# TensorE's convolution taps of a two-block model: fp32 products with one diagonal, or three fp32r products with rounded and remainder diagonals

## The chip, the cores and the metric

One core of one Trainium2 chip runs the whole program as one launch. The metric is the device time of the execution in microseconds, as the median of several runs of the kernel on one chip; less is better. Beside the runs there is one profiled execution, whose trace gives each instruction's start, length and engine.

## The reference, cut to what matters

The model has 1024 tokens of width 1024 and consists of three mixers with norms around them. The second, odd_mixer, is the one that the change touches:

```python
proj = h @ w_in                                   # 1024 -> 3 * 1024
a, b, gate = split(proj)
glu = a * sigmoid(b)
conv = depthwise_conv(glu, dw_w)                  # causal, 31 taps for each of 1024 channels
cf = conv + dw_b
cn = layer_norm(cf) * ln_g + ln_b
y = (silu(cn) * silu(gate)) @ w_out
x = x + rms_norm(y) * post_norm
```

Before it stands a mixer of windowed attention and pooling, after it a block with a third projection (to 3080 columns, with meta tokens in front), attention over all tokens, an output projection and a feed-forward part of 4096. All is computed in float32.

## The kernel before, in words

Activations lie with channels on the 128 partitions and tokens along the free axis, as 8 groups of 128 channels (KD = 8). From the first output projection up to the third input projection the tokens are worked in two halves of 512 (h = 0 and 1), so that one half's projection runs beside the other half's norms. The order of all work is written out by hand, engine by engine; engines wait for each other by semaphores, and each engine takes its own instructions in order.

**Projections.** An fp32 product is made of three fp32r ones: weights and activations are split into a rounded part (WH, XHM) and a remainder (WL, XLM), and `three` (L808) multiplies rounded by rounded, rounded by remainder and remainder by rounded. A job of one half is 8 channel groups by three matmuls of 128x512, 24 in all (half_job). Jobs of the third projection, first half, are "front jobs" (front_job): each covers the 16 meta tokens and 512 others as two pieces of 264 columns, 48 matmuls, in a ring bank and in one of banks 6 and 4. A PSUM ring of four banks holds the results of the jobs. A job p waits for `w_ready` to reach p + 1.

**Weights.** They pass through three slots in the order WORDER. SP loads the raw weights of job p; GpSimd issues a DMA of the rounded ones (`high`, L687) when job p - 3 has run, and computes the remainder (`low`, L694) of job p - 1. GpSimd's loop over p is: high(p), low(p - 1), additions due at p (`add_tap`, L749), diagonals due at p.

**The convolution** is shared by three engines. VectorE makes six of the eight groups by multiply-and-add, a tap at a time (`conv`, L2106 to L2110). Group 5 is made of products by ScalarE (`tap_products`, L1533) that GpSimd adds (L749). Group 4 is TensorE's: a tap is a matmul of the glu's columns, shifted by j, with a diagonal of 128x128 that holds the tap of each channel (`run_taps`, L1062), summed in bank 6. GpSimd makes a diagonal of the identity and a column of TAPW (`diagonals`, L738), in batches of 6, 5, 5, 5, 5, 5; a batch waits until the batch two before it has run, and lies in the first half's part of YG. ScalarE takes bank 6 with its bias (`group_out`, L1593).

**Where the taps stand.** First half: the batches run after jobs 8, 10, 12 and 14 of the second projection's first half (P_IN1A + i) and after jobs 0 and 2 of its second half (P_IN1B + i). Second half: all six batches run one after another between the gate jobs (P_GATEB + k) and the front jobs (P_IN2A + c). TensorE then makes five front jobs, the sum over channels for the mean (`mean1`, L1044, bank 5), three more front jobs, and the second output projection's second half.

**What stands around it.** On ScalarE: `sigmoid_b` takes the b part of a glu (L1540), half_hi rounds an activation (L1411), silu_gate takes a gate job (L1600), gate_b is a gate and then the products of group 5 that are due, front_copy takes an even front job as two copies of 264 columns (L1674, L1675). On VectorE: glu (L2094) multiplies in the a part, add_output (L2065, L2067) adds a normed output, scaled_lo (L2082, L1884) makes the third projection's inputs after the norm's broadcast (`half_wide`, L917, in the gates' job 5), front_product (L2239) takes an odd front job, mids (L2121) subtracts the mean. VectorE's order at the place is: scaled_lo for the first half, taps 12 to 30 of group 3, all of group 6, front_product(0), taps 0 to 13 of group 7, front_product(1), the rest of group 7, mids. Front job 2 waits for front_copy(0), front job 3 for front_product(0), which frees its second bank.

## Time and profile before

| what | value |
|---|---|
| median of 3 runs | 2202.93 us (2198.22 to 2207.03) |
| the profiled execution | 2204.82 us, span 2203.0 us |
| TensorE busy | 2128.3 us, 97% of the span |
| VectorE busy | 1116.0 us, 51% |
| ScalarE busy | 506.0 us, 23% |
| GpSimd busy | 760.3 us, 35% |
| mean granted TensorE clock | 0.982 |

The span runs from the first to the last instruction, and the execution's own time lies 1.8 us above it. Lines such as L808 are lines of the kernel before. "Busy" leaves out register, branch, semaphore and DMA-issuing instructions; matmuls overlap in the pipeline, so a row's mean length of one matmul is longer than its pace. In rows of a timeline the columns are start and length in us, engine, line, operation, output and inputs, count, and in brackets the engine's idle time before it and what ended it.

### The profile page before, as it was taken

What the parts mean: (1) busy time and instruction counts of PE and PEld (TensorE: products, weight loads), DVE (VectorE), ACT (ScalarE), POOL (GpSimd) and SP (SyncE); (2) the same over time, 40 slices, a digit from 0 to 9 for tenths busy, and PEclk for the clock granted to TensorE, in tenths of its full rate; (3) what the DMA queues carried; (4) which work ended last, traced back from release to release, by engine and by line L of the source; (5) the groups of instructions that cost most, each with busy time, mean ns of one, the idle gap of its engine ahead of it and who ended that gap; (6) DMA issues with size and microseconds to landing.
All of it is one profiled execution on the core that took longest, in us unless ns stands there. A gap on an engine that the chain in (4) does not pass through costs nothing.

```text
span 2203.0 us, 24066 instructions
## 1 busy us (share of the span) xinstructions
PE 2128.3 (97%) x9720; PEld 1675.2 (76%) x9720; DVE 1116.0 (51%) x1463; ACT 506.0 (23%) x832; POOL 760.3 (35%) x606
## 2 busy tenths in 40 slices
PE   7999999999999998989998999999999999999997
PEld 6887877777777767778886556777888888888886
DVE  6137563779999888151563676352322323313223
ACT  3002553421224413220111554111110100101102
POOL 3221015567767853434243000222222222222220
PEclk9999999999999998999999999999999999999999
DMA  4432017444544523447225442222222222222222
GB/s 178 138 116 72 25 60 246 172 153 143 176 160 154 171 96 115 157 151 246 77 79 142 90 92 78 101 96 77 96 96 96 96 96 96 96 96 96 96 96 105
DMA packets 71086, 259.85 MB, mean 118 GB/s; under 512 B 8961, under 2 KB 9217, under 8 KB 70209
## 3 DMA queue, kind: packets, MB, share of 16 engines
q1 hardware_dynamic: 40064, 148.69, 21.6%
q0 software_dynamic: 29808, 108.54, 13.7%
q8 instruction: 77, 1.26, 0.2%
q10 hardware_dynamic: 1104, 1.10, 0.2%
q14 instruction: 33, 0.26, 0.0%
HBM read 230.80 MB, written 12.65 MB: 111 GB/s over the span
## 4 chain that ended last, share of the span: by engine, by line
PE 59%; issue 28%; POOL 8%; DVE 4%; ACT 1%; DMA 1%; POOLq 0%; DVEq 0%; ACTq 0%
PE PS L808 55%; POOL WL L694 6%; DVE PS L2108 3%; PE PS L1062 2%; POOL WH L687 1%; DMA WH<-weights 1%; DVE OT L2511 0%; PE PS L917 0%; PE PS L1271 0%; PE PS L909 0%; ACT SQH L1533 0%; ACT PS L1618 0%; PE PS L1160 0%; DVE PS L2141 0%; ACT VX L1723 0%
## 5 line engine op out<-in xcount | busy, mean ns | idle before, releaser
L808 PE MATMUL PS<-XHM,WH 128*128 128x512 f32 (+1 forms) x1976 | 690.2, 391 | 24.9 <-DVE XLM L1884 12.3
L808 PE MATMUL PS<-XLM,WH 128*128 128x512 f32 (+1 forms) x1976 | 674.0, 382 | 0.0
L808 PE MATMUL PS<-XHM,WL 128*128 128x512 f32 (+1 forms) x1976 | 670.6, 381 | 0.0
L687 POOL DMA_DIRECT2D WH<-weights x207 | 119.2, 576 | 1323.7 <-PE PS L808 1305.5
L694 POOL TENSOR_TENSOR WL<-WRAW,WH 128x1024 fp32r<-128x1024 f32 x207 | 502.0, 2425 | 28.7 <-DMA WH<-weights 24.3
L808 PEld LDWEIGHTS PS<-XHM,WH 128*128 128x128 f32 x1976 | 368.5, 190 | 117.7 <-issue 22.9
L808 PEld LDWEIGHTS PS<-XLM,WH 128*128 128x128 f32 x1976 | 376.1, 190 | 79.8 <-issue 3.1
L808 PEld LDWEIGHTS PS<-XHM,WL 128*128 128x128 f32 x1976 | 375.5, 190 | 75.2
L2108 DVE SCALAR_TENSOR_TENSOR PS<-G,TAPW,PS 128x512 f32<-128x512 f32 x348 | 262.7, 755 | 11.7
L2489 DVE TENSOR_TENSOR X<-X,PS 128x1024 f32<-128x1024 f32 x64 | 78.2, 1222 | 243.5 <-PE PS L808 243.5
L2479 DVE SCALAR_TENSOR_TENSOR TM<-PS,RBM 128x1024 f32<-128x1024 f32 x32 | 39.1, 1225 | 246.4 <-PE PS L808 246.4
L1846 ACT ACTIVATE TM<-TM 128x1024 f32<-128x1024 f32 x32 | 33.9, 1061 | 550.3 <-DVE TM L2479 550.3
L808 PE MATMUL PS<-AL,WH 128*128 128x512 f32 x512 | 159.6, 393 | 0.0
L808 PE MATMUL PS<-AH,WH 128*128 128x512 f32 x512 | 158.8, 391 | 0.0
L808 PE MATMUL PS<-AH,WL 128*128 128x512 f32 x512 | 158.2, 390 | 0.0
L808 PEld LDWEIGHTS PS<-AH,WL 128*128 128x128 f32 x512 | 96.1, 188 | 22.0
L808 PEld LDWEIGHTS PS<-AL,WH 128*128 128x128 f32 x512 | 96.2, 188 | 20.9
L808 PEld LDWEIGHTS PS<-AH,WH 128*128 128x128 f32 x512 | 96.2, 188 | 20.3
L1229 PE MATMUL PS<-PT,VX 128*128 128x512 f32 (+4 forms) x224 | 86.0, 486 | 5.1 <-ACT PT L1773 5.1
L2472 DVE TENSOR_TENSOR AL<-TM,AH 128x1024 fp32r<-128x1024 f32 x32 | 84.3, 2655 | 1.1 <-ACT AH L1848 1.1
L749 POOL TENSOR_TENSOR RBM<-RBM,SQH 128x512 f32<-128x512 f32 x58 | 74.9, 1291 | 23.0 <-ACT SQH L1533 21.7
L1893 DVE TENSOR_TENSOR PS<-PS,SQH 128x512 f32<-128x512 f32 x60 | 41.6, 695 | 65.3 <-ACT SQH L1420 64.4
(253 smaller groups left out, 2084.8 us busy)
## 6 DMA issues: line engine op xcount, KB each, us to landing
WRAW<-weights SPq DMA_DIRECT2D x207, 512.0 KB, 3.5
WH<-weights POOLq DMA_DIRECT2D x207, 512.0 KB, 4.5
XTOK<-x SPq DMA_DIRECT2D x8, 512.0 KB, 7.6
x_kept<-X SPq DMA_DIRECT2D x4, 1024.0 KB, 7.6
X<-x_kept SPq DMA_DIRECT2D x8, 512.0 KB, 5.1
x_kept<-X SPq DMA_DIRECT2D x8, 512.0 KB, 8.6
X<-x_kept SPq DMA_DIRECT2D x2, 2048.0 KB, 9.6
out<-OT SPq DMA_DIRECT2D x8, 512.0 KB, 2.6
```

What stands on the lines that cost most here:

```text
L687: g.dma_start(WH[:, u, :], weights[WORDER[p]]).then_inc(w_hi[u], 16)
L694: g.tensor_tensor(WL[:, u, :], WRAW[:, u, :], WH[:, u, :].bitcast(F32), ALU.subtract)\
L749: g.tensor_tensor(dst, SSUMH[1], SQH[:, 1, i % 2, :], ALU.add).then_inc(tap_added, 1)
L808: m = nc.tensor.matmul(dst[:, a:b], w, v[:, a:b], start=first and n == 0, stop=last and n == 2)
L1062: m = nc.tensor.matmul(bank(6), diagonal(b, i - TAP_BATCH[part]), G1[:, c, h * HALF + j:(h + 1) * HALF + j], start=i == 0, stop=i == TAPS - 1,
L1229: m = nc.tensor.matmul(o[:, q0 - half * HALF:q0 - half * HALF + w], VX[0:keys, j, c, HD * e:HD * e + P], PT2[n % 3][0:keys, a:a + w], star ...
L1846: nc.scalar.activation(TM[:, j % 2, :], TM[:, j % 2, :], ACT.Square).then_inc(a_sq, 1)
L1893: v.tensor_tensor(so_far if k < KD - 1 else SSUMH[h], so_far, SQH[:, h, k % 2, :], ALU.add).then_inc(h_added[h], 1)
L2108: then(v.scalar_tensor_tensor(out=acc, in0=src, scalar=tap, in1=acc, op0=ALU.mult, op1=ALU.add))
L2472: v.tensor_tensor(AL[:, g % 2, j, :], TM[:, j % 2, :], AH[:, g % 2, j, :].bitcast(F32), ALU.subtract).then_inc(a_split, 1)
L2479: v.scalar_tensor_tensor(out=TM[:, j % 2, :], in0=slot(use + j), scalar=0.0, in1=RB[:], op0=ALU.max, op1=ALU.mult).then_inc(evacuated, 1)
L2489: v.tensor_tensor(X[:, e, :], X[:, e, :], slot(use + e), ALU.add).then_inc(evacuated, 1)
```

## The change

The tap as a float is split like the weights and activations of the projections. TAP2 holds, for the 31 taps of group 4, the rounded value and the remainder side by side (in the space of SMALL). ScalarE rounds the glu's columns into a strip (`tap_highs`): 542 columns as two strips of 286 (EDGE), and GpSimd subtracts the remainders (`tap_lows`). They lie in groups 4 to 7 of the first half's part of YG; the diagonals in groups 0 to 3. A tap is three fp32r matmuls: rounded diagonal by rounded strip, rounded by remainder, remainder by rounded; each reads its 512 columns as two pieces of 256, one in each strip. The product of the two remainders is left out.

A batch now has 4 taps (the last 3), so there are 8 in a half. GpSimd makes the four diagonals of two taps (two rounded, two remainders) in one two-input product of 128x512 with repeated elements, 16 instructions a half. tap_highs(0) stands on ScalarE behind the rounding of the second half's activations for the second projection, tap_lows(0) on GpSimd at P_IN1A + 8 behind low; the batches of the first half run on TensorE after jobs 10, 12, 14 and then 0, 2, 4, 6, 8. For the second half tap_highs(1) stands behind gate_b(4), tap_lows(1) at P_GATEB + 5, and the eight batches run in pairs behind front jobs 0 to 3, summed in bank 5. The waits for the inputs and for the first half's group stand before the front jobs; the wait for the second half's group stands before the mean. group_out(0) moves behind the fifth sigmoid of the second half, group_out(1) before the third front_copy.

The diff, with unchanged lines left out:

```diff
--- before.py
+++ after.py
@@ -68,7 +68,8 @@
...
 GLU_ORDER = (4, 5, 0, 1, 2, 3, 6, 7)
-TAP_BATCH = (0, 6, 11, 16, 21, 26, TAPS)
+TAP_BATCH = (*range(0, TAPS, 4), TAPS)
+NBATCH = len(TAP_BATCH) - 1
...
@@ -220,7 +221,9 @@
...
         RR = fixed("RR", [8, P])
+        o_small = top[0]
         SMALL = fixed("SMALL", [P, 96])
+        TAP2 = at("TAP2", [P, TAPS, 2], o_small, F32R)
         area = top[0]
...
@@ -241,6 +244,9 @@
...
         YG = at("YG", [P, KD, S], area + 33728)
+        YGR = at("YGR", [P, KD, S], area + 33728, F32R)
+        DIAG = at("DIAG", [P, KD, S // P, P], area + 33728, F32R)
+        EDGE = HALF // 2 + TAPS - 1
         SQH = at("SQH", [P, 2, 2, HALF], area + 66496)
...
@@ -368,6 +374,8 @@
...
         tap_added = sem("tap_added")
+        tap_hi = sem("tap_hi")
+        tap_lo = sem("tap_lo")
         diag_ready = sem("diag_ready")
...
@@ -500,9 +508,12 @@
...
-        def diagonal(b, n):
-            n += 6 * (b % 2)
-            return YG[:, n // 4, (n % 4) * P:(n % 4 + 1) * P]
+        def diagonal(b, n, e):
+
+            return DIAG[:, 2 * (b % 2) + n // 2, 2 * (n % 2) + e, :]
+
+        def tap_part(e, side):
+            return YGR[:, 4 + 2 * e + side, 0:EDGE]
...
@@ -723,20 +734,33 @@
...
+            def tap_lows(n):
+
+                c, h = TAP_GROUPS[n]
+                if n == 0:
+                    pool.wait_ge(tap_hi, 1)
+                    g.tensor_tensor(TAP2[:, :, 1], TAPW[:, c, :], TAP2[:, :, 0].bitcast(F32), ALU.subtract)\
+                        .then_inc(tap_lo, 1)
+                    pool.wait_ge(tap_lo, 1)
+                for side in range(2):
+                    first = h * HALF + side * HALF // 2
+                    pool.wait_ge(tap_hi, 2 + 2 * n + side)
+                    g.tensor_tensor(tap_part(1, side), G1[:, c, first:first + EDGE], tap_part(0, side).bitcast(F32),
+                                    ALU.subtract).then_inc(tap_lo, 1)
+
             def diagonals(b):
...
-                if b == 0:
-                    pool.wait_ge(taps_in, 16)
-                    pool.wait_ge(h_new[0], KD)
-                if b == 6:
-                    pool.wait_ge(h_new[0], 2 * KD)
+                n, part = divmod(b, NBATCH)
+                h = TAP_GROUPS[n][1]
                 if b >= 2:
                     pool.wait_ge(taps_run, b - 1)
-                (c, h), part = TAP_GROUPS[b // 6], b % 6
-                for i in range(TAP_BATCH[part], TAP_BATCH[part + 1]):
-                    j = taps_of(h)[i]
-                    g.tensor_scalar(diagonal(b, i - TAP_BATCH[part]), IDENT[:], TAPW[:, c, j:j + 1], None, ALU.mult)\
-                        .then_inc(diag_ready, 1)
+                for i in range(TAP_BATCH[part], TAP_BATCH[part + 1], 2):
+                    j, taps = taps_of(h)[i], min(2, TAPS - i)
+                    row = 2 * (b % 2) + (i - TAP_BATCH[part]) // 2
+                    pairs = TAP2[:, j:j + taps, :].rearrange("p t e -> p (t e)").bitcast(F32)
+                    g.tensor_tensor(DIAG[:, row, 0:2 * taps, :],
+                                    IDENT[:].unsqueeze(1).broadcast_to((P, 2 * taps, P)),
+                                    pairs.unsqueeze(2).broadcast_to((P, 2 * taps, P)), ALU.mult).then_inc(diag_ready, 1)
...
@@ -748,8 +772,10 @@
...
-            BUILT = {P_IN1A + 4: (0,), P_IN1A + 6: (1,), P_IN1A + 11: (2,), P_IN1A + 13: (3,), P_IN1A + 15: (4,),
-                     P_IN1B + 1: (5,), P_GATEB + 6: (6, 7), P_IN2A + 2: range(8, 12)}
+            BUILT = {P_IN1A + 9: (0,), P_IN1A + 11: (1,), P_IN1A + 13: (2,), P_IN1A + 15: (3,), P_IN1B + 1: (4,),
+                     P_IN1B + 3: (5,), P_IN1B + 5: (6,), P_IN1B + 7: (7,), P_GATEB + 6: (8,), P_GATEB + 7: (9,),
+                     P_IN2A + 2: (10, 11), P_IN2A + 3: (12, 13), P_IN2A + 4: (14, 15)}
+            LOWS = {P_IN1A + 8: 0, P_GATEB + 5: 1}
...
@@ -758,6 +784,8 @@
...
                         add_tap(n)
+                if p in LOWS:
+                    tap_lows(LOWS[p])
                 for b in BUILT.get(p, ()):
...
@@ -1049,19 +1077,19 @@
...
-                n, part = divmod(b, 6)
+                n, part = divmod(b, NBATCH)
                 c, h = TAP_GROUPS[n]
+                acc = bank((6, 5)[n]).rearrange("p (s t) -> p s t", s=2)
                 if part == 0:
                     pe.wait_ge(x_split, (X_IN1[1], X_IN2[0])[h] + KD)
-                    wait_freed(pe, (N_A, c, h))
-                    if n >= 1:
-                        pe.wait_ge(group_ready, n)
-                pe.wait_ge(diag_ready, TAPS * n + TAP_BATCH[part + 1])
+                    pe.wait_ge(tap_lo, 3 + 2 * n)
+                pe.wait_ge(diag_ready, (TAPS + 1) // 2 * n + (TAP_BATCH[part + 1] + 1) // 2)
                 for i in range(TAP_BATCH[part], TAP_BATCH[part + 1]):
                     j = taps_of(h)[i]
-                    m = nc.tensor.matmul(bank(6), diagonal(b, i - TAP_BATCH[part]),
-                                         G1[:, c, h * HALF + j:(h + 1) * HALF + j], start=i == 0, stop=i == TAPS - 1,
-                                         skip_group_check=True)
+                    for t, (ed, ev) in enumerate(((0, 0), (0, 1), (1, 0))):
+                        m = nc.tensor.matmul(acc, diagonal(b, i - TAP_BATCH[part], ed),
+                                             YGR[:, 4 + 2 * ev:6 + 2 * ev, j:j + HALF // 2], start=i == 0 and t == 0,
+                                             stop=i == TAPS - 1 and t == 2, skip_group_check=True)
                 m.then_inc(taps_run, 1)
...
@@ -1097,12 +1125,12 @@
...
                         half_wide(1, H_PRE1)
-                    if i >= 8 and i % 2 == 0:
-                        run_taps((i - 8) // 2)
+                    if i >= 10 and i % 2 == 0:
+                        run_taps((i - 10) // 2)
                 for i in range(10):
                     half_job(P_IN1B + i, ((N_B, N_A)[i % 2], GLU_ORDER[i // 2], 1), X_IN1[1] if i == 0 else None)
-                    if i in (0, 2):
-                        run_taps(4 + i // 2)
+                    if i % 2 == 0:
+                        run_taps(3 + i // 2)
                 for k in range(KD):
...
@@ -1119,15 +1147,18 @@
...
                     half_job(P_GATEB + k, (N_G, k, 1), None, hooks)
-                for b in range(6, 12):
-                    run_taps(b)
                 pe.wait_ge(m_split, 1)
-                pe.wait_ge(group_ready, 2)
+                pe.wait_ge(group_ready, 1)
+                pe.wait_ge(x_split, X_IN2[0] + KD)
                 for c in range(8):
...
                               X_IN2[0] if c == 0 else None, hooks)
+                    if c < 4:
+                        run_taps(NBATCH + 2 * c)
+                        run_taps(NBATCH + 2 * c + 1)
                     if c == 4:
+                        pe.wait_ge(group_ready, 2)
                         mean1(1, 0, KD)
...
@@ -1572,6 +1603,19 @@
...
+            def tap_highs(n):
+
+                c, h = TAP_GROUPS[n]
+                if n == 0:
+                    nc.scalar.activation(TAP2[:, :, 0], TAPW[:, c, :], ACT.Copy).then_inc(tap_hi, 1)
+                act.wait_ge(h_new[0], KD * (n + 1))
+                wait_freed(act, (N_A, c, h))
+                if n >= 1:
+                    act.wait_ge(taps_run, NBATCH * n)
+                for side in range(2):
+                    first = h * HALF + side * HALF // 2
+                    nc.scalar.activation(tap_part(0, side), G1[:, c, first:first + EDGE], ACT.Copy).then_inc(tap_hi, 1)
+
             half_root(1, H_POST0)
...
@@ -1582,6 +1626,8 @@
...
             scaled_hi(1, H_PRE1, range(4, KD))
+            act.wait_ge(taps_in, 16)
+            tap_highs(0)
             tap_products(P_IN1A + 6)
...
@@ -1589,8 +1635,8 @@
...
                 c, h = TAP_GROUPS[n]
-                act.wait_ge(taps_run, 6 * (n + 1))
-                nc.scalar.activation(G1[:, c, conv_out(h)], bank(6), ACT.Identity,
+                act.wait_ge(taps_run, NBATCH * (n + 1))
+                nc.scalar.activation(G1[:, c, conv_out(h)], bank((6, 5)[n]), ACT.Identity,
                                      bias=GAINS[:, G_DWB, c:c + 1]).then_inc(group_ready, 1)
...
@@ -1627,8 +1673,7 @@
...
                 tap_products(P_IN1B + 2 * i)
-                if i == 2:
-                    group_out(0)
+            group_out(0)
             act.wait_ge(x_split, X_IN1[1] + KD)
...
@@ -1660,13 +1705,12 @@
...
             gate_b(4)
+            tap_highs(1)
             scaled_hi(0, H_MIX, range(4))
...
             gate_b(7)
-            group_out(1)
-
             def front_copy(c, dst):
...
@@ -1682,6 +1726,8 @@
...
                 act.wait_ge(cf_ready[1], c + 1)
+                if c == 2:
+                    group_out(1)
                 front_copy(2 * c, CU[:, c, :])
...
                 if c == 2:
```

## Rows read from the trace of the kernel before

**Rows 1.** the page, busy time by engine, and VectorE's convolution taps

```profile
PE 2128.3 (97%) x9720; PEld 1675.2 (76%) x9720; DVE 1116.0 (51%) x1463; ACT 506.0 (23%) x832; POOL 760.3 (35%) x606
...
L2108 DVE SCALAR_TENSOR_TENSOR PS<-G,TAPW,PS 128x512 f32<-128x512 f32 x348 | 262.7, 755 | 11.7
```

**Rows 2.** chain of waits, 430 to 930 us: start, length, what

```profile
470.23 5.15 PE PS L1062 x12
...
475.38 11.12 PE PS L808 x48
...
580.31 0.69 DVE G L2094
...
658.04 2.40 POOL WL L694
...
781.43 26.61 PE PS L1062 x62
...
808.87 17.66 PE PS L808 x144
```

**Rows 3.** VectorE's waits in 550 to 600 us, and its timeline

```profile
DVE G L2094 <- PE PS L808: 3.1, 3, 1.9
...
815.05 0.75 DVE L2110 SCALAR_TENSOR_TENSOR G<-G,TAPW,PS 128x512 f32<-128x512 f32 x1
...
820.81 0.43 DVE L2239 TENSOR_TENSOR G<-PS,G 128x264 f32<-128x264 f32 x1 [5.00 <-PE PS L808]
```

**Rows 4.** TensorE's timeline: start, length, what, idle before

```profile
660.48 0.50 PE L808 MATMUL PS<-XHM,WH 128*128 128x512 f32 x1 [1.09 <-POOL WL L694]
...
838.18 6.17 PE L1044 MATMUL PS<-G,ONES 128*128 128x512 f32 x14
...
846.78 1.12 PE L1044 MATMUL PS<-G,ONES 128*128 128x512 f32 x2 [2.42 <-DVE G L2110]
```

**Rows 5.** GpSimd's groups by line and shape: count, busy, mean ns

```profile
L694 POOL TENSOR_TENSOR WL<-WRAW,WH 128x1024 fp32r<-128x1024 f32 x207 | 502.0, 2425 | 28.7 <-DMA WH<-weights 24.3
...
L749 POOL TENSOR_TENSOR RBM<-RBM,SQH 128x512 f32<-128x512 f32 x58 | 74.9, 1291 | 23.0 <-ACT SQH L1533 21.7
...
L738 POOL TENSOR_SCALAR YG<-IDENT,TAPW 128x128 f32<-128x128 f32 x62 | 36.2, 596 | 5.7 <-PE PS L1062 5.7
```

**Rows 6.** GpSimd's timeline, two weight remainders of the second projection, jobs 7 and 8

```profile
454.44 2.43 POOL L694 TENSOR_TENSOR WL<-WRAW,WH 128x1024 fp32r<-128x1024 f32 x1
...
460.00 2.42 POOL L694 TENSOR_TENSOR WL<-WRAW,WH 128x1024 fp32r<-128x1024 f32 x1
```

**Rows 7.** ScalarE's timeline, three places

```profile
463.66 0.81 ACT L1528 ACTIVATE RBM<-G,GAINS,TAPW 128x512 f32<-128x512 f32 x1
...
763.29 0.60 ACT L1600 ACTIVATE YG<-PS 128x512 f32<-128x512 f32 x1 [3.00 <-PE PS L808]
...
763.78 0.71 ACT L1533 ACTIVATE SQH<-G,TAPW 128x512 f32<-128x512 f32 x1
...
815.01 0.38 ACT L1674 COPY G<-PS 128x264 f32<-128x264 f32 x1 [6.24 <-PE PS L808]
```

**Rows 8.** TensorE's timeline, the broadcast in job 5 of the gates

```profile
763.88 1.15 PE L917 MATMUL PS<-RT,ROWSEL 8*128 8x128 f32 x8
```

**Rows 9.** DMA issues of the page: KB, us from issue to landing

```profile
WH<-weights POOLq DMA_DIRECT2D x207, 512.0 KB, 4.5
```

**Rows 10.** a long wait, and stretches with the granted clock (PEclk, third last)

```profile
1206.23 0.77 PE L1207 MATMUL PS<-QQ,KK 128*128 128x512 f32 x1 [5.12 <-DMA KK<-KL]
...
1206.00:1208.00 2.00, 1.77 (x5) 1.07 (x5) 0.00 (x0) 0.42 (x1) 1.53 (x4) 0.50 1.05 235
...
1208.00:1210.00 2.00, 2.00 (x5) 0.98 (x4) 0.00 (x0) 0.68 (x2) 1.89 (x1) 0.52 1.04 234
...
848.00:850.00 2.00, 2.00 (x12) 2.00 (x11) 1.89 (x3) 1.26 (x3) 0.00 (x0) 0.53 0.00 0
```

## The prediction, made before the changed kernel ran

> **What bounds the kernel now.** The page's busy line first [rows 1]: TensorE is busy 2128.3 of 2203.0 us, VectorE 1116.0, GpSimd 760.3. That says TensorE bounds the kernel, and it is an average. The change touches only two stretches, 430 to 600 us and 745 to 850 us, so the chain of waits is read there [rows 2]. It runs on TensorE until 580 us; then VectorE has it through its own convolution taps (the group of 348 at 755 ns in [rows 1]), a weight remainder of GpSimd (L694) sits in it at 658 us, and TensorE's taps of the second half are in it with 26.6 us. Next, who waited for whom. VectorE waited for TensorE 3.1 us between 550 and 600 us, and once for 5.0 us at 820.81 us, for the second front job [rows 3]. TensorE waited for VectorE's last convolution group before the mean, 2.42 us at 846.78 us [rows 4]. So in both stretches the two engines are within 2 to 5 us of each other: what TensorE saves beyond VectorE's waits is lost, and VectorE cannot gain more than 3.1 + 5.0 = 8.1 us.
>
> **Taps on TensorE.** A tap is now one fp32 matmul of two instructions: 62 of them in 26.61 us [rows 2], 0.858 us a tap, 26.6 us a half. It becomes three fp32r matmuls. The projection's fp32r matmuls of 128x512 run 48 in 11.12 us [rows 2], 0.2317 us each, so 0.695 us a tap, 21.5 us a half. Saved: 5.1 us a half, 10.2 us in all. No row shows an fp32r matmul that reads at odd columns or in two pieces of 256. Bounds: 0.2317 us from the rows nearest in type, 0.429 us from the fp32 tap instruction, which reads at odd columns. I take 0.2317, since type, size and weight load are the same.
>
> By the Trainium skill ("FP8 and Floating Point Precision", TensorE Precision Notes) an fp32 product is four passes, so three would save a quarter, an estimate of 13.3 us in all; the rows give 10.2, because an fp32 pass takes 0.2145 us and an fp32r matmul 0.2317. By the page, TensorE would be 1.6 us earlier after each half, and the sum below about 1.6 us smaller.
>
> **Diagonals on GpSimd.** Before, 31 one-input products of 128x128 a half at 0.596 us, 18.5 us. Now 16 two-input products of 128x512: a tap addition or remainder of that form takes 1.291 us [rows 5], so 20.7 us. Lower bound 1.29; upper bound 4 x 0.596 = 2.38 us, should a read that repeats elements run at the old product's rate. I take 1.29, the row of the same operation and size.
>
> **Remainders on GpSimd, the new waits.** tap_lows makes GpSimd wait for ScalarE and then subtracts two strips of 286 columns. From 1.291 us at 512 and 2.425 us at 1024 columns [rows 5], a strip is an estimated 0.79 us. Behind it in GpSimd's queue stand a weight DMA issue (0.58 us) and the remainder of the next projection's weights (2.42 us), for which TensorE waits. That is the step that costs.
>
> First half: GpSimd ends the weights of job 7 at 456.9 us and did those of job 8 at 460.00 us [rows 6]. Now it waits in between for tap_highs, which ScalarE reaches at 463.66 us [rows 7], behind the last rounded half. Small copy 0.2 us, strip copies about 0.3 us apart (a 264-column copy takes 0.38 us in [rows 7]); GpSimd's second strip ends at about 465.9, issue 466.5, weights 468.9 us. TensorE begins job 8 at 470.23 - 24 x 0.2317 = 464.7 us. **Stall 4.2 us.**
>
> Second half: tap_highs stands behind gate_b(4), which waits for job 4 of the gates; tap_lows stands before the weights of job 5. So TensorE must stall, whatever its pace. Gate at 763.29, product at 763.78 [rows 7], copies from 764.4, second strip done 766.4, issue 767.0, weights 769.4 us; job 5 began at about 763.2, its three matmuls before the broadcast at 763.88 [rows 8]. **Stall 6.2 us.** The weight DMAs behind are late too: they land 4.5 us after issue [rows 9], and with two batches of diagonals at 2.6 us among them, the gates' jobs 6 and 7 are ready when TensorE is, to within 0.5 us.
>
> **Clock.** After TensorE's 5.12 us wait at 1206.23 us the granted clock was 0.50 (1.2 GHz) up to 1208 us and 0.52 on the mean up to 1210 us [rows 10]: some 3.6 us of work at half speed, 1.8 us lost. In job 5 of the gates the three matmuls and the broadcast before VectorE's part take 1.8 us at full speed [rows 8], so they fit in such a stretch. I charge 1.6 us after each stall; bounds 0 (it doesn't fall) and 1.8.
>
> **Sum, first half.** The new order has three taps fewer before the seventh late job (28 of 31), so there TensorE stands at -26.6 + 28 x 0.695 + 4.2 + 1.6 = -1.3 us. VectorE needed 3.1 and gets 1.3. At the job that waited 1.09 us for weights at 660.48 us [rows 4], TensorE stands at -5.1 + 5.8 = +0.7, while the weights come 1.3 earlier; it could start at 659.4 (1.09 before) and now starts at 660.1. Gain 0.4 us, carried to 763 us, where TensorE runs through.
>
> **Sum, second half.** The broadcast for the next norm, and with it VectorE, comes 6.2 + 1.6 - 0.4 = 7.4 us later. VectorE then has the third projection's inputs to scale and convolution taps up to 815.8 us, where it waited 5.0 us [rows 3]. Front job 1 now ends at about 805.9 us, so this wait takes up 5.0: +2.4 us. TensorE, with that 0.4 us: job 5 runs from 769.0 to 777.3 (5.56 + 1.1 for the broadcast + 1.6). GpSimd meanwhile does an addition 1.3, a batch 2.6, an issue 0.6 and weights 2.4, in all 6.9 us, and again for the next: weights at 775.9 and 782.8, jobs 6 and 7 end at 782.9 and 788.5. Then fronts of 5.9 us (3 in 17.66, [rows 2]), each of the first three with two batches of taps (8 x 0.695 = 5.6) behind it: front 1 ends at 805.9, front 2 at 817.4, its taps at 823.0. In such a round of 11.5 us GpSimd has two batches, issue, weights and addition, 9.5 us, and keeps up. Front 3 waits for VectorE's first product until 824.0, last taps (7) 834.8, front 4 840.7 (before, 838.18, [rows 4]), seven sums of the mean 846.9. VectorE's last group comes at 849.1. Slack 2.2 us, so VectorE decides. Everything after follows the mean. ScalarE's five copies hide in its waits (it sat idle 3.0 and 6.2 us there, [rows 7]), and so does group_out. SP's loads are not moved; they run up to three jobs ahead.
>
> Sum: -0.4 + 6.2 + 1.6 - 5.0 = **+2.4 us**, against 2204.82 us of the profiled execution. That one lies 1.9 us above the median of 2202.93, so 2205.3 us.
>
> **Rivals.**
> *The clock does not fall.* First half gain 2.0 (TensorE at -0.9 where the weights were awaited, start at 658.5), second half 6.2 - 5.0 = 1.2 loss: -0.8 us, 2202.1 us. For it: a wait of 1.09 us changed nothing; against it, both stalls are longer than the 2.42 us after which it fell to 0.53 [rows 4, 10].
> *VectorE's waits go in full.* If the copies reach GpSimd without a stall, both waits vanish: -8.1 us, 2194.8 us. Against: the queue orders above.
> *GpSimd's products cost 2.38 us.* A batch is 4.8 us; from 1.6 us an instruction on, front 4 comes after VectorE. Two batches lie before the weights of jobs 6 and 7, 2 x 2.2 = 4.4 us later; then a round takes GpSimd 13.8 us against TensorE's 11.5, which eats its lead and adds some 3 us by the last batches. Front 4 ends at 847.9, the mean's 7.0 us at 854.9 against 847.9: +7.0 us, 2209.9 us. For it: the old one-input product is slow per element, 0.596 us for 128. By the Trainium skill ("GPSIMD Engine Reference", Elementwise) a two-input operation is the slower, 2.6 against 1.8 cycles an element, which by an estimate from the old product would be 3.4 us; [rows 5] show the opposite, 1.29 us for 512.
> *Slower: TensorE's shifted reads.* Where: run_taps. If the fp32r matmul runs at 0.429 us when it reads at odd columns, each half costs 18.4 us more; the first comes through whole, the second less its slack, and the sum above remains: 18.4 + 18.4 - 2.2 + 2.4 = +37.0 us, 2239.9 us. It decides from 0.255 us on (2.2 us over 93 matmuls). Against: fp32 reads at odd columns run at 0.2145 us a pass.
> *The change doesn't do what it says* (an fp32r product becomes two instructions): priced as the last.
>
> **Numbers.** Forecast 0.57; clock 0.13; waits gone 0.12; GpSimd 0.10; shifted reads 0.05; not named 0.03. The range 2196 to 2213 takes in the first two, most of the next two, and the clock and strip bounds. A measurement of this kernel tells about 0.5% (11 us) from no change. No named case is faster by that: 0.02. Slower: shifted reads and part of the unnamed and of GpSimd's: 0.08. Same 0.90.
>
> **What would show it.** TensorE waits for a weight remainder (L694's successor) of some 4 us near 465 and 6 us near 763 us, with half clock after; taps at 0.232 us; products of 1.3 us; VectorE's 5.0 us wait gone; mean still waiting about 2 us for VectorE. Wrong if TensorE shows no wait at the gates' job 5, or if front 4 ends after VectorE's last group.

## The result, and the profile after

| | before | after |
|---|---|---|
| median of 15 runs each, same chip | 2203.13 us | 2207.91 us (2204.88 to 2211.07) |
| ratio | | 1.0021, interval 1.0013 to 1.0029 |
| profiled execution, span | 2204.82, 2203.0 us | 2209.2, 2207.4 us |
| mean granted TensorE clock | 0.982 | 0.981 |

The change costs 4.8 us; the forecast was 2205.3 us, a cost of 2.4. The line numbers have moved: `three` is L836 (L808 before), the weight remainder L705 (L694), the weight DMA L698 (L687), the taps L1090 (L1062), the mean L1072 (L1044), VectorE's convolution L2154 and L2156 (L2108, L2110), its glu L2140 (L2094), its front_product L2285 and L2286, the broadcast L945 (L917).

The page of after, busy time by engine, and three groups (count, busy, mean ns, idle before them), as in [rows 1, 5]:

```profile
PE 2120.7 (96%) x9782; PEld 1687.2 (76%) x9782; DVE 1113.9 (50%) x1463; ACT 507.7 (23%) x837; POOL 760.1 (34%) x581
...
L2154 DVE SCALAR_TENSOR_TENSOR PS<-G,TAPW,PS 128x512 f32<-128x512 f32 x348 | 262.7, 755 | 11.7
...
L748 POOL TENSOR_TENSOR YGR<-G,YGR 128x286 fp32r<-128x286 f32 x4 | 3.1, 793 | 8.6 <-ACT YGR L1617 8.5
...
L761 POOL TENSOR_TENSOR DIAG<-IDENT,TAP 128x512 fp32r<-128x512 f32 x30 | 30.6, 1039 | 9.0 <-PE PS L1090 9.0
```

TensorE is busy 7.6 us less than before and the kernel is 4.8 us slower, within 0.1% to 0.3% by the interval. TensorE's timeline of after (start, length, what, idle before) says where the time went, and answers to [rows 2, 4, 8]:

```profile
466.42 0.79 PE L836 MATMUL PS<-XHM,WH 128*128 128x512 f32 x1 [4.18 <-POOL WL L705]
...
568.26 2.96 PE L1090 MATMUL PS<-YGR,DIAG 128*128 128x512 f32 x12
571.06 0.39 PE L836 MATMUL PS<-XHM,WH 128*128 128x512 f32 x1
...
766.98 0.80 PE L836 MATMUL PS<-XHM,WH 128*128 128x512 f32 x1 [6.13 <-POOL WL L705]
...
768.56 2.07 PE L945 MATMUL PS<-RT,ROWSEL 8*128 8x128 f32 x8
...
823.45 0.36 PE L836 MATMUL PS<-XHM,WH 128*128 128x264 f32 x1 [1.02 <-DVE G L2286]
...
848.50 2.08 PE L1072 MATMUL PS<-G,ONES 128*128 128x512 f32 x2 [2.26 <-DVE G L2156]
```

The two stalls stand where they were forecast, with 4.18 and 6.13 us for 4.2 and 6.2. The batch of four taps takes 571.06 - 568.26 = 2.80 us for 12 matmuls, 0.233 us each: columns at odd places and in two pieces cost nothing that shows beside the 0.2317 of [rows 2]. The mean still waits for VectorE, 2.26 us for the 2.42 of [rows 4].

GpSimd's timeline of after, the queue that makes the stalls ([rows 6] before):

```profile
452.02 2.42 POOL L705 TENSOR_TENSOR WL<-WRAW,WH 128x1024 fp32r<-128x1024 f32 x1
461.54 0.26 POOL L742 TENSOR_TENSOR TAP<-TAPW,TAP 128x31 fp32r<-128x31 f32 x1 [7.09 <-ACT TAP L1610]
461.93 1.54 POOL L748 TENSOR_TENSOR YGR<-G,YGR 128x286 fp32r<-128x286 f32 x2
463.41 0.57 POOL L698 DMA_DIRECT2D WH<-weights  x1
464.01 2.36 POOL L705 TENSOR_TENSOR WL<-WRAW,WH 128x1024 fp32r<-128x1024 f32 x1
...
748.90 2.43 POOL L705 TENSOR_TENSOR WL<-WRAW,WH 128x1024 fp32r<-128x1024 f32 x1
...
762.50 1.53 POOL L748 TENSOR_TENSOR YGR<-G,YGR 128x286 fp32r<-128x286 f32 x2 [8.48 <-ACT YGR L1617]
763.98 0.57 POOL L698 DMA_DIRECT2D WH<-weights  x1
764.57 2.35 POOL L705 TENSOR_TENSOR WL<-WRAW,WH 128x1024 fp32r<-128x1024 f32 x1
```

GpSimd sits idle 7.09 and 8.48 us for ScalarE's copies, with the weights that TensorE wants queued behind. Next VectorE's timeline at the gates, a row of before and then two of after, and ScalarE's of after:

```profile
765.13 1.41 DVE L2082 SCALAR_TENSOR_TENSOR PS<-X,GAINS,PS 128x512 f32<-128x512 f32 x2 [1.05 <-PE PS L917]
...
770.72 1.41 DVE L2128 SCALAR_TENSOR_TENSOR PS<-X,GAINS,PS 128x512 f32<-128x512 f32 x2 [9.04 <-PE PS L945]
...
778.78 0.69 DVE L1930 TENSOR_TENSOR XLM<-PS,XHM 128x512 fp32r<-128x512 f32 x1 [1.01 <-ACT XHM L1442]
```

```profile
777.05 0.60 ACT L1646 ACTIVATE YG<-PS 128x512 f32<-128x512 f32 x1 [1.42 <-PE PS L836]
777.55 0.71 ACT L1564 ACTIVATE SQH<-G,TAPW 128x512 f32<-128x512 f32 x1
778.16 1.08 ACT L1442 ACTIVATE XHM<-PS 128x512 fp32r<-128x512 f32 x2
```

VectorE's wait for the broadcast has grown by 9.04 - 1.05 = 8.0 us. And there is a wait that the forecast does not have: ScalarE's gate_b(5) stands ahead of the second half of scaled_hi, and waits for the stalled gate job until 777.05 us. VectorE's remainders need ScalarE's rounding (L1442 at 778.16) and wait 1.01 us.

The granted clock of after (third number from the end), by stretches of 2 us:

```profile
466.00:468.00 2.00, 1.58 (x4) 1.29 (x5) 1.89 (x4) 0.00 (x0) 2.00 (x3) 0.56 0.56 199
468.00:470.00 2.00, 2.00 (x7) 1.56 (x6) 1.93 (x3) 0.00 (x0) 1.98 (x3) 0.59 0.23 41
470.00:472.00 2.00, 2.00 (x11) 1.60 (x10) 1.89 (x4) 0.00 (x0) 2.00 (x2) 1.00 0.66 221
...
766.00:768.00 2.00, 1.02 (x3) 0.83 (x3) 0.00 (x0) 0.00 (x0) 2.00 (x2) 0.50 0.56 203
...
770.00:772.00 2.00, 2.00 (x6) 1.49 (x6) 1.28 (x2) 0.49 (x1) 1.98 (x3) 0.50 0.20 39
772.00:774.00 2.00, 2.00 (x7) 1.61 (x6) 1.96 (x4) 1.05 (x3) 2.00 (x2) 0.64 0.63 227
```

It fell to 1.2 GHz after both stalls, as forecast. After the second it stays there until the matmuls take 0.4 us again at about 773.3 us: 6.3 us of work from 766.98, where the forecast charges 1.6 us for the part ahead of the broadcast and nothing for the rest of the job.

**Two stretches as sums.** The first stage of this trace, where nothing was changed, ran 2.42 us shorter (GpSimd's remainder for job 7 of the second projection starts at 452.02 for 454.44 us). The granted clock differs there between the two profiles: before it was 0.50 in 60 to 62 and in 190 to 192 us, in after 1.00 in both. So I compare distances. From the remainder for the gates' job 4 (748.90 us) to the last two matmuls of the mean (848.50) it is 99.60 us; before it was 846.78 - 751.30 = 95.48 (751.30 us is the start of the same remainder in the trace of before). The second half costs **+4.1 us**. From 452.02 to 748.90 it is 296.88, before 296.86: the first half gives **0.0 us**.

### The profile page after: what moved, and what is told of

Same layout as the page of the kernel before. It is cut to its first block, busy times and chain, and to the rows that moved or that the text cites. A ratio compares the mean times of both kernels' runs of the same rounds, so it can differ in the third digit from the quotient of the medians.

```text
span 2207.4 us, 24172 instructions
## 1 busy us (share of the span) xinstructions
PE 2120.7 (96%) x9782; PEld 1687.2 (76%) x9782; DVE 1113.9 (50%) x1463; ACT 507.7 (23%) x837; POOL 760.1 (34%) x581
## 4 chain that ended last, share of the span: by engine, by line
PE 61%; issue 28%; POOL 8%; DVE 1%; DMA 1%; ACT 1%; POOLq 0%; DVEq 0%; ACTq 0%
PE PS L836 57%; POOL WL L705 6%; PE PS L1090 2%; POOL WH L698 1%; DMA WH<-weights 1%; DVE OT L2557 0%; PE PS L945 0%; PE PS L1302 0%; PE PS L1072 0%; PE PS L937 0%; ACT PS L1664 0%; PE PS L1191 0%; ACT SQH L1564 0%; DVE PS L2187 0%; ACT XHM L1442 0%
## 5 line engine op out<-in xcount | busy, mean ns | idle before, releaser
L836 PE MATMUL PS<-XHM,WH 128*128 128x512 f32 (+1 forms) x1976 | 687.6, 389 | 35.8 <-POOL WL L705 13.6
L836 PE MATMUL PS<-XLM,WH 128*128 128x512 f32 (+1 forms) x1976 | 673.3, 382 | 0.0
L836 PE MATMUL PS<-XHM,WL 128*128 128x512 f32 (+1 forms) x1976 | 669.8, 380 | 0.0
L698 POOL DMA_DIRECT2D WH<-weights x207 | 119.6, 578 | 1314.7 <-PE PS L836 1292.7
L705 POOL TENSOR_TENSOR WL<-WRAW,WH 128x1024 fp32r<-128x1024 f32 x207 | 502.5, 2428 | 24.4 <-DMA WH<-weights 20.1
L836 PEld LDWEIGHTS PS<-XHM,WH 128*128 128x128 f32 x1976 | 368.2, 190 | 127.1 <-issue 21.0
L836 PEld LDWEIGHTS PS<-XLM,WH 128*128 128x128 f32 x1976 | 375.7, 190 | 78.9 <-issue 2.0
L836 PEld LDWEIGHTS PS<-XHM,WL 128*128 128x128 f32 x1976 | 375.0, 190 | 75.6
L2154 DVE SCALAR_TENSOR_TENSOR PS<-G,TAPW,PS 128x512 f32<-128x512 f32 x348 | 262.7, 755 | 11.7
L836 PE MATMUL PS<-AL,WH 128*128 128x512 f32 x512 | 159.5, 393 | 0.0
L836 PE MATMUL PS<-AH,WH 128*128 128x512 f32 x512 | 158.7, 391 | 0.0
L836 PE MATMUL PS<-AH,WL 128*128 128x512 f32 x512 | 158.2, 390 | 0.0
L836 PEld LDWEIGHTS PS<-AH,WL 128*128 128x128 f32 x512 | 96.1, 188 | 22.0
L836 PEld LDWEIGHTS PS<-AL,WH 128*128 128x128 f32 x512 | 96.2, 188 | 20.9
L836 PEld LDWEIGHTS PS<-AH,WH 128*128 128x128 f32 x512 | 96.2, 188 | 20.3
```

Of the source, the lines that this page charges most:

```text
L698: g.dma_start(WH[:, u, :], weights[WORDER[p]]).then_inc(w_hi[u], 16)
L705: g.tensor_tensor(WL[:, u, :], WRAW[:, u, :], WH[:, u, :].bitcast(F32), ALU.subtract)\
L836: m = nc.tensor.matmul(dst[:, a:b], w, v[:, a:b], start=first and n == 0, stop=last and n == 2)
L2154: then(v.scalar_tensor_tensor(out=acc, in0=src, scalar=tap, in1=acc, op0=ALU.mult, op1=ALU.add))
```

## The experiments

The theory after the result: two queue orders (GpSimd's remainders behind ScalarE's copies; VectorE behind the stalled gate job) cost what TensorE's shorter taps and VectorE's old wait give back, and more. The rival: TensorE's taps or GpSimd's products, the new work itself. Ratios are against runs of the kernel before on the same chip; a difference in us behind one is the ratio less 1, times 2203 us. Code that an excerpt doesn't show is that of after.

**Both groups of remainders one place later on GpSimd** (6 runs).

```diff
-            LOWS = {P_IN1A + 8: 0, P_GATEB + 5: 1}
+            LOWS = {P_IN1A + 9: 0, P_GATEB + 6: 1}
```

> Both blocks of remainder strips (tap_lows) stand one job later in GpSimd's loop, behind the weights that TensorE asks for next. Theory A (the loss is the two stalls for weights; VectorE's order decides the mean): the 6.1 us stall shrinks to under 2 us and moves to the gates' jobs 6 and 7, where TensorE has slack; VectorE is no longer delayed by 9.0 us before it scales the third projection's inputs, its old 5.0 us wait for front job 1 stays gone; the first half gives up to 2.0 us more. Against the kernel before: -5 to -7 us, ratio 0.997 to 0.998. Rival B (the taps among the front jobs cost the time, by TensorE or by GpSimd's products between the weights): the ratio stays at 1.001 to 1.002. Rival C (the profiled local balance is right but the rest of the program drifts by some 2 us on its own): the ratio moves by less than 3 us.

Measured: 2195.65 us, 0.9955 (0.9939 to 0.997), -9.9 us. TensorE's timeline of this run at the jobs behind the two that had stalled, and at the mean:

```profile
470.61 0.50 PE L836 MATMUL PS<-XHM,WH 128*128 128x512 f32 x1 [0.72 <-POOL WL L705]
...
768.82 0.50 PE L836 MATMUL PS<-XHM,WH 128*128 128x512 f32 x1 [1.39 <-POOL WL L705]
...
839.16 1.12 PE L1072 MATMUL PS<-G,ONES 128*128 128x512 f32 x2 [1.44 <-DVE G L2156]
```

Both stalls are gone; one job later TensorE waits 0.72 us and, at the gates, 1.39. The rival is refuted by this run alone: TensorE's taps and GpSimd's products are all there, and the kernel is faster than before. The gain is outside the 5 to 7 us expected. In the two stretches the trace shows 2.3 + 5.0 = 7.3 us; no row gives the rest to the edit (see the end of the next section). I ran it once more, beside a later run (5 runs):

> The run with both groups of remainders one place later, once more on the same chip as the next one. Its first measurement was 0.9955 of the kernel before, 0.9 percentage points below the changed kernel. If that gap is the edit's own, this one again lies between 0.993 and 0.998 of the kernel before (2188 to 2199 us). If a part of it was chance, it is 0.998 to 1.000.

Measured: 2196.71 us, 0.996 (0.9946 to 0.9974), -8.8 us. The gap to the changed kernel repeats: 0.66 and 0.61 percentage points (the 0.9 in the expectation is a slip). One line of GpSimd's order turns a cost of 5 us into a gain of 9 to 10.

**Only the second group later** (9 runs).

```diff
-            LOWS = {P_IN1A + 8: 0, P_GATEB + 5: 1}
+            LOWS = {P_IN1A + 8: 0, P_GATEB + 6: 1}
```

> Only the second half's strips one job later, the first half's as in the changed kernel. Theory A: the 4.2 us stall near 466 us stays and costs what it cost, the gates' stall is gone, so -4 to -5.5 us against the kernel before and 0.5 to 2 us more than with both moved. Rival: if the first stall is what costs, the time stays at +3 to +5 us.

Measured: 2198.10 us, 0.9968 (0.9956 to 0.9979), -7.0 us, more than the 4 to 5.5 expected. So of the 13 to 14.5 us between the changed kernel and the runs above, 11.7 go with the gates' stall and 2 to 3 with the first. The stretch from the gates to the mean shows 9.1 of the 11.7; the other 2.6 lie outside it.

**One product a tap** (12 runs). Leaves out rounded diagonal by remainder strip and remainder diagonal by rounded strip, so the convolution of group 4 is computed from rounded values alone.

```diff
-                    for t, (ed, ev) in enumerate(((0, 0), (0, 1), (1, 0))):
+                    for t, (ed, ev) in enumerate(((0, 0),)):
...
-                                             stop=i == TAPS - 1 and t == 2, skip_group_check=True)
+                                             stop=i == TAPS - 1, skip_group_check=True)
```

> Leaves out two of the three products of each of TensorE's taps (only rounded by rounded is computed), all else as in the changed kernel, so TensorE has 14.4 us less in each half. Theory A: VectorE's order decides the mean of the second half, so nothing is gained there, the sum of the mean only waits for VectorE some 17 us instead of 2.3; in the first half VectorE's wait of 2.05 us for a glu goes and TensorE is early where it was late, together at most 3.1 us. Against the kernel before +1 to +3 us, against the changed one -2 to -3. Rival B (TensorE's work decides): -20 us or more against the changed kernel.

Measured: 2209.45 us, 1.0021 (1.0011 to 1.0031), the same as after, where 2 to 3 us less were expected: a miss. 124 matmuls of 0.2317 us, 28.7 us of TensorE's work, are gone, and nothing comes of it. TensorE's waits in this run, 600 to 860 us (total, times, longest), and GpSimd's timeline:

```profile
PE PS L836 <- POOL WL L705: 18.0, 3, 11.1
PE PS L836 <- DVE G L2286: 12.3, 1, 12.3
PE PS L1072 <- DVE G L2156: 2.9, 1, 2.9
```

```profile
652.83 1.27 POOL L773 TENSOR_TENSOR RBM<-RBM,SQH 128x512 f32<-128x512 f32 x1 [14.65 <-ACT SQH L1564]
654.04 0.57 POOL L698 DMA_DIRECT2D WH<-weights  x1
654.63 2.37 POOL L705 TENSOR_TENSOR WL<-WRAW,WH 128x1024 fp32r<-128x1024 f32 x1
```

TensorE waits 11.1 us for the remainder that stands at 658.04 us before [rows 2]. GpSimd has an addition ahead of it, which waits for a product of ScalarE, and ScalarE has stood idle 23.3 us for VectorE's centred convolution, as its own timeline has it:

```profile
646.32 0.60 ACT L1451 ACTIVATE PS<-G 128x512 f32<-128x512 f32 x1 [23.26 <-DVE G L2167]
...
652.04 0.71 ACT L1564 ACTIVATE SQH<-G,TAPW 128x512 f32<-128x512 f32 x1
```

Whatever TensorE saves, this remainder comes at 654.6, 3.1 us earlier when the traces' starts are lined up. In the second half the saving goes into 12.3 us for front_product. So TensorE's taps are not what costs. The 3.1 us are there at this remainder, but only 1.5 are left at the gates: TensorE's clock falls behind the 11.1 us wait too, and over the whole program the mean of its 12 runs is 0.974 where the 15 of after have 0.981. What was taken from TensorE's work became idle time, and part of it came back as a slower clock.

**A filler in the two stalls** (12 runs): 15 and 22 matmuls of the identity by itself, in fp32, into columns that the job then overwrites.

```diff
-                pe.wait_ge(w_ready, p + 1)
                 if n >= 4:
                     wait_freed(pe, JOBS[n - 4])
+                for _ in range({P_IN1A + 8: 15, P_GATEB + 5: 22}.get(p, 0)):
+                    nc.tensor.matmul(ring(job)[:, 0:P], IDENT[:], IDENT[:], start=True, stop=True)
+                pe.wait_ge(w_ready, p + 1)
```

> TensorE multiplies the identity by itself into the job's own free bank while it waits for weights in the two stalls (15 and 22 small fp32 matmuls, some 3.2 and 4.7 us, inside stalls of 4.2 and 6.1 us). Theory A with the clock: the granted clock stays at 1.00 after both stalls; the three matmuls and the broadcast in the gates' job 5 take 1.8 us, not 3.4, so VectorE starts 1.6 us earlier; with the first half's part 2 to 3 us less than the changed kernel. Rival (the clock falls in any case, or its cost is hidden): the time stays within 0.5 us of the changed kernel.

Measured: 2204.62 us, 1.0000 (0.9991 to 1.0009): 4.7 us less than after, by the ratios, more than the 2 to 3 expected. The clock in this run's windows stays up, and VectorE's wait at the gates (745 to 851 us: total, times, longest) shrinks from 9.0 us:

```profile
466.00:468.00 2.00, 1.80 (x17) 1.61 (x15) 1.91 (x3) 0.00 (x0) 1.98 (x2) 1.00 0.83 272
...
768.00:770.00 2.00, 2.00 (x13) 1.47 (x12) 0.42 (x1) 0.00 (x0) 2.00 (x3) 1.00 0.03 8
```

```profile
DVE PS L2130 <- PE PS L947: 7.5, 1, 7.5
DVE G L2169 <- PE PS L1074: 2.1, 1, 2.1
```

The 1.0 us wait for ScalarE is gone too, since the gate job ends earlier. In the two stretches the trace shows 1.7 + 2.7 = 4.4 us less than after. So the slow clock behind the stalls costs 4 to 5 us, the wait for ScalarE included, where the forecast charged 3.2; the two ratios by themselves leave 2 to 7.

**The second half's batches in one block, with the remainders later** (11 runs).

```diff
-                     P_IN2A + 2: (10, 11), P_IN2A + 3: (12, 13), P_IN2A + 4: (14, 15)}
+                     P_IN2A + 2: range(10, 16)}
-            LOWS = {P_IN1A + 8: 0, P_GATEB + 5: 1}
+            LOWS = {P_IN1A + 9: 0, P_GATEB + 6: 1}
...
+                for b in range(NBATCH, 2 * NBATCH):
+                    run_taps(b)
...
-                    if c < 4:
-                        run_taps(NBATCH + 2 * c)
-                        run_taps(NBATCH + 2 * c + 1)
```

> As e1 (strips one job later), but all eight batches of the second half run before front job 0, as the fp32 taps did, not in pairs among the fronts. Theory: TensorE's 21.5 us of taps instead of 26.6 bring front job 1 some 5 us earlier, so VectorE's 5.0 us wait for it almost goes either way; the place among the fronts is worth about 1 us: 1 to 3 us slower than e1, -7 to -9 us against the kernel before. Rival (the place is the gain): back to -2 to -5 us against before.

Measured: 2198.21 us, 0.9976 (0.9966 to 0.9985), -5.3 us (-7.5 to -3.3). That lies between the theory's 7 to 9 and the rival's 2 to 5, so the time decides for neither. By the ratios it is 3.5 and 4.6 us behind the two runs with pairs, by the medians 1.5 and 2.6. The trace places it: VectorE waits 2.4 us for front job 1, and the second half is 2.6 us shorter than before where the pairs give 5.0. Both the place and the shorter taps are needed.

**The kernel before, its fp32 taps in pairs among the front jobs** (11 runs), summed in bank 5. The taps and the first half are those of before; GpSimd makes the last two batches one job later, and group_out(1) moves as in after.

```diff
-                     P_IN1B + 1: (5,), P_GATEB + 6: (6, 7), P_IN2A + 2: range(8, 12)}
+                     P_IN1B + 1: (5,), P_GATEB + 6: (6, 7), P_IN2A + 2: (8, 9), P_IN2A + 3: (10, 11)}
...
+                    if c < 3:
+                        run_taps(6 + 2 * c)
+                        run_taps(7 + 2 * c)
...
-                for b in range(6, 12):
-                    run_taps(b)
...
```

> The kernel before, with the fp32 taps and its one-element-wide diagonals, but the second half's six batches in pairs behind front jobs 0 to 2 and in the fifth bank; no strips, so no new wait. Theory: VectorE's 5.0 us wait for front job 1 goes; TensorE reaches front job 4's end when it did before, 838 us, so the seven sums of the mean end at 844.4 and TensorE no longer waits there, VectorE does: the mean comes about 2.5 us earlier, and since TensorE has no wait at the mean the clock doesn't fall after it: -2 to -4 us against the kernel before. Rival (all of e1's gain is the place): -8 us or more. Rival (the place gives nothing without faster taps): within 1 us.

Measured: 2200.06 us, 0.9987 (0.9977 to 0.9996), -2.9 us, within the 2 to 4 expected, but not in the expected way: VectorE's wait for front job 1 does not go, it is 3.7 us for 5.0 before, and TensorE still waits 2.43 us at the mean. The interleaving alone is worth 1.3 us by the trace, not 2.5. The rest of the 2.9 stands where nothing was changed (0.9 us in the first half, 2.7 behind the mean), so that the time came out right is in part luck.

**ScalarE's copies earlier instead** (6 runs), with GpSimd's second group later too.

```diff
+            act.wait_ge(taps_in, 16)
+            tap_highs(0)
             sigmoid_b(0, 3)
             scaled_hi(1, H_PRE1, range(4, KD))
-            act.wait_ge(taps_in, 16)
-            tap_highs(0)
...
             half_root(0, H_MIX)
+            tap_highs(1)
             gate_b(4)
-            tap_highs(1)
```

> ScalarE rounds the strips earlier (the first half's before the fourth sigmoid, the second half's behind the root of the third norm, before gate 4), and GpSimd subtracts at P_IN1A + 8 and P_GATEB + 6. Theory: no wait of TensorE for weights near 465 us nor in the gates' jobs 5 to 7; against e1 0 to 2 us less, -10 to -12 us against the kernel before, 0.9945 to 0.9955. Rival (ScalarE's 0.76 us of copies delay the chain of the norm): not faster than e1.

Measured: 2196.70 us, 0.9963 (0.9949 to 0.9977), -8.1 us, for an expected 10 to 12; as the rival has it, though not for its reason, not better than the first. The first half shows why. TensorE's timeline and the clock of this run:

```profile
656.68 0.79 PE L836 MATMUL PS<-XHM,WH 128*128 128x512 f32 x1 [2.80 <-POOL WL L705]
```

```profile
656.00:658.00 2.00, 1.32 (x3) 1.12 (x4) 1.86 (x4) 1.98 (x5) 1.40 (x2) 0.50 1.09 408
658.00:660.00 2.00, 2.00 (x6) 1.52 (x6) 1.89 (x4) 1.07 (x1) 1.98 (x3) 0.50 0.30 53
```

TensorE comes earlier to the remainder that cannot come earlier, waits 2.8 us, and the clock is at half for some 6 us behind it: 3 us lost again. At the gates this kernel is 0.4 us ahead of before, where the first had 2.3 and 2.8.

**The sixth gate behind the rounding** (one run).

```diff
             scaled_hi(0, H_MIX, range(4))
-            gate_b(5)
             scaled_hi(0, H_MIX, range(4, KD))
+            gate_b(5)
```

> The changed kernel with gate 5 behind the rounding of all of the third projection's inputs on ScalarE. One look at the trace: theory, VectorE's new wait of 1.01 us for a rounded input near 778 us comes from gate 5, which waits for the stalled job 5, and is gone; TensorE's last sum of the mean comes 1.0 us earlier relative to the broadcast in job 5. Rival: the wait stays, it comes from ScalarE's pace.

Measured: 2201.67 us, a single run, so only its stage is read. VectorE's wait for ScalarE's rounding is gone and its 9.0 us for the broadcast remains; the second half costs 3.0 us for the 4.1 of after. The unforecast wait is worth what it shows.

**Both groups later, and the second half's copies ahead of the gate** (5 runs).

```diff
-            LOWS = {P_IN1A + 8: 0, P_GATEB + 5: 1}
+            LOWS = {P_IN1A + 9: 0, P_GATEB + 6: 1}
...
             half_root(0, H_MIX)
+            tap_highs(1)
             gate_b(4)
-            tap_highs(1)
```

> Both groups of remainders one place later, and ScalarE's copies of the second half ahead of the gate that waits for TensorE; the first half's copies stay where they are. Theory (queue order): TensorE's remaining wait of 1.4 us at the gates goes, since GpSimd's strips no longer come behind a gate's sigmoid; the mean still waits for VectorE, whose own start moves up with TensorE's broadcast by that 1.4 us. So 0 to 1.5 us below the run beside it, about 2195 us. Rival (knock-on): as with both halves' copies early, the work moved up meets a late weight remainder elsewhere, and the time is 0 to 2 us above.

Measured: 2195.61 us, 0.9956 (0.9943 to 0.997), -9.7 us, beside 2196.71 for the run without that move: no difference that these runs resolve. The trace speaks against my theory of it: TensorE's 1.4 us wait at the gates is gone, and yet the second half is 5.0 us shorter than before in both. VectorE waits 1.0 us for the broadcast in both as well, so it was not late and there was nothing to move up.

**All runs by one sum.** The second half's length against before should be what VectorE waits there, less the 1.0 + 5.0 us that it waited before. VectorE's three waits are for the broadcast, for ScalarE's rounding and for a front job. The first half's should be VectorE's wait in its glu (4.0 us before, from 440 to 600 us), read where the remainder of 658.04 us stands.

| kernel | VectorE's waits, second half | sum less 6.0 | second half measured |
|---|---|---|---|
| after | 9.0 + 1.0 + 0 | +4.0 | +4.1 |
| one product | 9.0 + 1.9 + 0 | +4.9 | +5.1 |
| sixth gate behind | 9.0 + 0 + 0 | +3.0 | +3.0 |
| filler | 7.5 + 0 + 0 | +1.5 | +1.4 |
| before, taps among fronts | 1.0 + 0 + 3.7 | -1.3 | -1.3 |
| later, one block | 1.1 + 0 + 2.4 | -2.5 | -2.6 |
| the five others | 1.0 + 0 + 0 | -5.0 | -5.0 each |

| kernel | VectorE's glu wait | less 4.0 | remainder at 658.04, measured |
|---|---|---|---|
| after | 2.9 | -1.1 | -1.0 |
| second group later | 4.0 | 0 | +0.1 |
| sixth gate behind | 4.1 | +0.1 | +0.2 |
| before, taps among fronts | 4.0 | 0 | 0.0 |
| filler | 1.4 | -2.6 | -2.5 |
| the six others | 0.9 | -3.1 | -3.0 to -3.1 |

The second table's remainder is measured from each trace's remainder of job 7. The sums hold to 0.2 us in all eleven profiles. So VectorE bounds what the two tables measure, in every kernel here: what TensorE saves counts only as far as it shortens one of these waits. The first half's stretch is longer than the second table, up to the gates. There TensorE decides where it comes too late to wait for the remainder of 658.04 us, in after, second group later, sixth gate behind and filler: its sums for the first half's mean start 1.1, 2.2 and 2.4 us later than before and 0.3 earlier, counted from the remainder of job 7.

## Why the prediction was right, and where it was off

**The verdict and the case.** Within 0.5%, by the forecast case, and 2.6 us above the forecast, inside the range. The clock fell (against the first rival). The rival in which both waits go without a stall failed too: the copies came as late as the queue orders said, both stalls stood, and only 1.1 of the first wait's 3.1 us went. GpSimd's products did not slow down, they took 1.02 us each (2.04 for two at 466.32 us; the group's mean above is 1.04) for my 1.29 and the rival's 2.38. The shifted reads ran at 0.233 us for 0.2317.

By the Trainium skill ("GPSIMD Engine Reference", Elementwise) the two-input product would be the dearer for each element. The trace has 1.04 us for 512 elements against 0.596 us for 128, so the 3.4 us estimated from the old product did not come; as the two differ in size, it does not tell an element's price from what each instruction costs by itself. By the Trainium skill ("FP8 and Floating Point Precision", TensorE Precision Notes) an fp32 product's four passes would make three products a quarter cheaper; at 0.233 us a matmul TensorE saved 0.858 - 0.70 = 0.16 us a tap, less than a fifth.

**The stalls**: 4.18 and 6.13 us for 4.2 and 6.2. Queue order and neighbouring rows were enough for both. The strips took 0.793 us for an estimated 0.79.

**VectorE's old wait, -5.0**: gone in full, and the mean decided by VectorE with 2.26 us of slack for 2.2.

**First step that was off: "gain 0.4 us, carried to 763 us".** At the gates' job 4 it is 0.0 in this trace, and in two more with the same first half 0.0 (second group later) and +1.2 lost (sixth gate behind). VectorE got 1.1 us of the forecast 1.3. In the trace of after the first stall's clock cost what was charged: 0.56 and 0.59 for 4 us, 1.7 lost for 1.6. But TensorE is 1.1 us late at the first half's mean, for the forecast 0.7, and starts its next sums (L937) 208.80 us behind the remainder of job 7 for 209.01 before: 0.2 ahead, for the forecast 0.4. The 0.2 go at the first job of the second output projection, where TensorE waits 0.5, 1.1 and 1.1 us for VectorE's remainders and the clock falls in before and in after, in after one matmul earlier. The step has no term for this. The windows of before and of after behind these waits, then that of the taps among fronts, where the clock does not fall and the stretch is 0.9 us shorter:

```profile
688.00:690.00 2.00, 2.00 (x6) 1.50 (x6) 1.93 (x4) 0.00 (x0) 0.00 (x0) 0.50 0.00 0
```

```profile
685.00:687.00 2.00, 2.00 (x5) 1.61 (x6) 1.97 (x3) 0.00 (x0) 0.00 (x0) 0.50 0.00 0
```

```profile
687.00:689.00 2.00, 2.00 (x9) 1.43 (x9) 1.97 (x3) 0.38 (x1) 0.00 (x0) 1.00 0.00 0
```

The clock behind the first stall varies as well. I took 1.8 us as the upper bound of its cost, but in the trace of the sixth gate behind:

```profile
466.00:468.00 2.00, 1.43 (x3) 1.16 (x4) 1.89 (x4) 0.00 (x0) 2.00 (x3) 0.50 0.65 205
...
470.00:472.00 2.00, 2.00 (x6) 1.52 (x6) 1.89 (x4) 0.00 (x0) 2.00 (x2) 0.50 0.69 250
472.00:474.00 2.00, 2.00 (x9) 1.61 (x8) 1.93 (x3) 0.00 (x0) 0.68 (x1) 0.88 0.00 0
```

The work starts at 466.57 and runs at half speed to about 472.3: 5.7 us, 2.9 lost. The 3.6 us of [rows 10] is one sample of a length that varies from run to run. The bound should have been wider. With the second group later the two effects cancel: 1.1 us more lost behind the stall than in after, nothing lost at the first job of the output projection.

**Second step: "the broadcast, and with it VectorE, comes 6.2 + 1.6 - 0.4 = 7.4 us later".** It is 8.0 us, 0.2 above the 7.8 that the step has without the 0.4.

**Third step: what it does not list.** The forecast asks for GpSimd and TensorE what is queued behind an added wait, not for ScalarE: gate_b(5) waits for the stalled job and holds up scaled_hi, +1.0 us. The clock has a part in it: the job ran at half speed for 6.3 us, 3.1 lost for the 1.6 charged, and in the filler run, where it did not, this wait is gone.

**The sum.** The terms of the profiled trace: 0.4 (first half) + 0.2 + 1.0 + 0.1 (unplaced) = 1.7, from +2.4 to the +4.1 that the trace shows at the mean. Median against median it is +4.8, and the profiled executions differ by 4.4 = -2.4 (the first stage) + 0.0 + 4.1 + 2.7 behind the mean. I don't read more into the last 0.7 than that.

**What stays open.** From the mean's last matmuls to the end of the span there are 1356.2 us before and 1350.3 to 1359.6 in the eleven other profiles, though nothing was changed there. Where the clock fell at the mean it is 1356.2 (before), 1358.9 (after), 1359.6 (one product) and 1358.5 us (filler); in the eight profiles where it stayed at full it is 1350.3 to 1356.9, 1353.9 on the mean. But the clock falls at other places of this stretch too, in other places in each profile. Counted over the whole stretch it is at half for 34 us where the length is 1350.3, for 41 where it is 1350.8, for 47 to 58 where it is 1353.5 to 1358.9, and for 61 where it is 1359.6; over the twelve profiles length and busy time at half clock go together with a correlation of 0.88. Runs of one kernel show the same without a profile: the 26 runs of before on the chip of the first experiments lie between 2200.1 us at a mean clock of 0.986 and 2208.0 at 0.981 (correlation -0.76; -1 would be a straight line downwards), the 15 of after likewise (-0.85). In the nine runs of before beside the last two experiments, all within 3.3 us, it doesn't show.

So what the two stretches don't explain goes largely with the clock, in the best kernels too: of their gain of 9 to 10 us the second half has 5.0. The first half has 2.3, 2.8 and 3.9 in their three profiles, with the clock at half for 3.4 us in the first two jobs of the second output projection in two of them and at full in the third. Whether the kernels with fewer stalls get a faster clock behind the mean, or had luck in 5 and 6 runs, no run isolates.

## What to carry to other kernels

An instruction that waits for another engine costs its wait to all that is queued behind it. Before a wait is put into a queue that feeds the bounding engine, list what stands behind it, and compare the position one place later: here that was one line and some 13 us, of which the two stretches show 11. If a stall cannot be avoided, list also the third engines that serve the stalled one in order.

A tuned stretch that two engines share has a floor that the busy time does not show. Take the waits of the second engine before as the ceiling of any gain on the first: 3.1 and 5.0 us here, against 28.7 us of work removed for nothing. And before a difference of 1 to 3 us between two profiles is given a cause, the granted clock of both is compared in the stretches where nothing was changed: the first stage here differed by 2.4 us with it.
